# A two-stage encoder block with product-key experts: the first expert table of the last 128 tokens as dot products with fetched rows

## The reference, cut to what matters

```python
def block(tb):                                    # 128 tokens
    qry = (tb @ w_q).reshape(PEER_BLOCK, PEER_HEADS, 2, PEER_HALF)
    s = jnp.einsum('thpd,pkd->thpk', qry, sub_keys)
    sv, si = lax.top_k(s, PEER_TOPK)
    ...
    top, pos = lax.top_k(cand, PEER_TOPK)
    eidx = jnp.take_along_axis(cidx, pos, axis=-1)
    gates = jax.nn.softmax(top.astype(jnp.float32), axis=-1)
    z = jnp.einsum('thed,td->the', expert_u[eidx], tb)
    act = (gates * jax.nn.gelu(z.astype(jnp.float32))).astype(tb.dtype)
    return jnp.einsum('the,thed->td', act, expert_v[eidx])
```

## Time and profile before

| | us |
|---|---|
| runs | 4876.5, 4875.06, 4876.28 (median 4876.28) |
| the profiled execution | 4867.86 |
| its span in the trace | 4866.3 |
| mean granted clock of TensorE | 0.991 of full speed |

### The profile page before, as it was taken

One profiled execution on the slowest core, in us unless ns is written; L12 is line 12 of the kernel. 1 busy time (PEld: TensorE's weight loads), 2 busy tenths in 40 slices (PEclk: granted clock), 3 DMA queues, 4 the chain that ended last, 5 costly groups with the idle time before them and its releaser, 6 DMA issues.

```text
span 4866.3 us, 67163 instructions
## 1 busy us (share of the span) xinstructions
PE 4750.8 (98%) x24576; PEld 4118.7 (85%) x24576; DVE 3004.8 (62%) x4220; ACT 1304.4 (27%) x1287; POOL 698.4 (14%) x741
## 2 busy tenths in 40 slices
PE   8999999999999999999999999999999879999998
PEld 6787888998998888877788888888888879999998
DVE  5555556666665433488788886222224368888886
ACT  4222222212223312212233333222222222223222
POOL 1111110000002001111000000000004732212223
PEclk9999999999999999999999999999999989999999
DMA  4444444555546633322333344333335468888884
GB/s 174 156 162 151 158 156 165 197 196 192 198 144 212 209 135 118 141 78 103 116 142 142 142 177 179 142 118 119 119 119 191 151 236 329 313 326 324 339 305 149
DMA packets 271844, 878.64 MB, mean 181 GB/s; under 512 B 20000, under 2 KB 169920, under 8 KB 197664
## 3 DMA queue, kind: packets, MB, share of 16 engines
q1 hardware_dynamic: 229520, 669.94, 38.3%
q0 software_dynamic: 42256, 207.85, 11.6%
HBM read 802.09 MB, written 209.78 MB: 208 GB/s over the span
## 4 chain that ended last, share of the span: by engine, by line
PE 90%; POOL 3%; DVE 2%; issue 2%; DMA 1%; ACT 0%; DVEq 0%; POOLq 0%; ACTq 0%; SPq 0%
PE bank L632 28%; PE bank L633 28%; PE bank L634 28%; POOL z_pairs L611 3%; DMA w_raw<-v_blocks 1%; PE bank L844 1%; PE bank L732 1%; PE bank L739 1%; DVE w_lo L1252 1%; PE bank L708 1%; PE bank L730 0%; ACT w_hi L905 0%; POOL cand L575 0%; DVE r L1800 0%; PE bank L670 0%
## 5 line engine op out<-in xcount | busy, mean ns | idle before, releaser
L632 PE MATMUL bank<-x_hi,w_hi 128*128 128x512 f32 (+1 forms) x5760 | 2081.1, 361 | 7.1 <-DVE w_lo L1252 7.1
L633 PE MATMUL bank<-x_lo,w_hi 128*128 128x512 f32 (+1 forms) x5760 | 2077.9, 361 | 0.0
L634 PE MATMUL bank<-x_hi,w_lo 128*128 128x512 f32 (+1 forms) x5760 | 2071.7, 360 | 0.0
L905 ACT ACTIVATE w_hi<-w_raw 128x2048 fp32r<-128x2048 f32 x432 | 827.3, 1915 | 2118.4 <-PE bank L634 2066.2
L1252 DVE TENSOR_TENSOR w_lo<-w_raw,w_hi 128x2048 fp32r<-128x2048 f32 x432 | 995.2, 2304 | 542.9 <-ACT w_hi L905 530.8
L632 PEld LDWEIGHTS bank<-x_hi,w_hi 128*128 128x128 f32 x5760 | 1082.9, 188 | 201.5 <-issue 21.3
L633 PEld LDWEIGHTS bank<-x_lo,w_hi 128*128 128x128 f32 x5760 | 1082.4, 188 | 172.1 <-issue 2.6
L634 PEld LDWEIGHTS bank<-x_hi,w_lo 128*128 128x128 f32 x5760 | 1084.0, 188 | 169.6
L632 PE MATMUL bank<-x_hi_o,w_hi 128*128 128x384 f32 x2048 | 687.1, 336 | 63.2 <-DVE w_lo L1252 63.2
L633 PE MATMUL bank<-x_lo_o,w_hi 128*128 128x384 f32 x2048 | 686.1, 335 | 0.3 <-issue 0.3
L634 PE MATMUL bank<-x_hi_o,w_lo 128*128 128x384 f32 x2048 | 686.0, 335 | 0.3 <-issue 0.3
(11 more groups left out here) (263 smaller groups left out, 2665.2 us busy)
## 6 DMA issues: line engine op xcount, KB each, us to landing
v_rows<-v_blocks SPq DMA_DIRECT2D x128, 1024.0 KB, 7.1
w_raw<-u_blocks SPq DMA_DIRECT2D x128, 1024.0 KB
w_raw<-v_blocks SPq DMA_DIRECT2D x128, 1024.0 KB
w_raw<-w_proj SPq DMA_DIRECT2D x112, 1024.0 KB
z_scratch<-z_stage POOLq DMA_DIRECT2D x128, 256.0 KB, 2.3
g_scratch<-g_chunk SPq DMA_DIRECT2D x6, 4096.0 KB, 12.3
z_group<-z_scratch SPq DMA_DIRECT2D x14, 1536.0 KB
g_group<-g_scratch SPq DMA_DIRECT2D x14, 1536.0 KB
```

What stands on the lines that cost most here:

```text
L632: pe.matmul(dst, whi, xhi, start=start, stop=False)
L633: pe.matmul(dst, whi, xlo, start=False, stop=False)
L634: return pe.matmul(dst, wlo, xhi, start=False, stop=stop)
L905: act.activation(WH[s][:, :], RAW[s][:, :], ACT.Copy).then_inc(w_hi, 1)
```

## The change

The last 128 tokens leave the Z stage as they had left the O stage. Their z values become dot products: VectorE multiplies a fetched row of the first table with the token's x row and sums it (`dot`), 128 times. For that:

- The first table is turned to rows in DRAM (`u_rows`), beside the projections: SP loads each of 128 tiles into a free buffer, VectorE transposes it in blocks of 32 x 32 (`u_turn`), SP stores it in four parts (`u_turned`). There is one buffer pair at a time, in four places (a1, a2, b2, c1): 38 tiles in A1, 61 in A2 and the first blocks of B1, 15 in B2 and C1, 14 in C1 and Q1. SP's loops are written out.
- The row copies of the second table are spread anew: one per block of A1, one per two blocks of A2, two per block of B1, one per block of Q1. The sub keys are loaded after A2.
- Z moves 384 columns. x of the last tokens is scaled (ScalarE, Q1), turned by 16 transposes (TensorE, after z block 5) and copied to `x_rows`.
- GpSimd fetches row sets into three buffers, three ahead of the dots. `dots(n)` puts one dot behind each z block 16 to 63 and a second one behind every eighth; after that nine per six blocks, to block 113. The gelu of all pairs is one activation, scaled with a column of 1/rms, before the gelu of z block 120.
- The one-hot products are in fp32, with 128 columns and no low part; the adds from PSUM go; chunks are 32 tokens.
- The 128 pair fetches go. Group 0 is loaded at z block 65, group 1 and the stored h by SP after the last dot. `V_FIRST` is 1. The last tokens' sums, norm and output are separate (`v_sums`, `h_rows`), and the other tokens' final steps have 384 columns.

```diff
-CH = 64
+CH = 32
...
-V_FIRST, V_LAST = 16, 119
+V_FIRST, V_LAST = 1, 119
+QD = P // 32
+U_A1, U_A2, U_B2, U_C1 = 0, 38, 99, 114
+U_A1_X, U_A2_X, U_B2_X, U_C1_X = 6, 52, B2 + 4, C1 + 4
+D_GATE, D_LATE = 9, 9
...
-    z_dram = nc.dram_tensor("z_scratch", (NB_E, P, T), F32, kind="Internal").ap()
+    z_dram = nc.dram_tensor("z_scratch", (NB_E, P, NT), F32, kind="Internal").ap()
...
+    u_rows = nc.dram_tensor("u_rows", (KEYS, QD, 32, QD, KT * 32), F32, kind="Internal").ap()
...
+        def dots(n):
+
+            if n < Z_LOOK + Z_GATE:
+                q, r = divmod(n - Z_LOOK, 8)
+                return [D_GATE * q + r] + ([D_GATE * q + 8] if r == 7 else [])
+            q, r = divmod(n - Z_LOOK - Z_GATE, 6)
+            p0 = D_GATE * Z_GATE // 8 + D_LATE * q
+            return [p for p in range(p0 + 3 * r // 2, p0 + 3 * (r + 1) // 2) if p < P]
...
+            def row_copy(n):
+                jg, d = n // GJ, n % GJ
+                src = v_blocks[n, :, :].rearrange("i (j c) -> i j c", j=GJ)
+                sp.dma_start(v_rows[jg, :, :, d, :], src).then_inc(vr_st, 16)
+
+            def weights(src, n, b0):
+                sp.wait_ge(w_lo, b0 + n + 1)
+                sp.dma_start(RAW[n % 2][:, :], src[n]).then_inc(w_loaded[n % 2], 16)
+
+            def u_load(m, bufs):
+                sp.dma_start(bufs[0][:, :], u_blocks[m]).then_inc(ur_ld, 16)
+
+            def u_turned(m, bufs, more):
+
+                sp.wait_ge(ur_turn, m + 1)
+                for b in range(QD):
+                    sp.dma_start(u_rows[m, b, :, :, :].rearrange("r a n -> a r n"), bufs[1][:, b * D // QD:(b + 1) * D // QD]
+                                 ).then_inc(ur_st[b], 16)
+                if more:
+                    u_load(m + 1, bufs)
+
+            for n in range(2, NB_A1 + NB_A2):
+                weights(w_proj, n, A1)
+                x = n - 2
+                if n < 50:
+                    row_copy(n - 2)
+                elif n % 2 == 0:
+                    row_copy(48 + (n - 50) // 2)
+                if x == U_A1_X - 1:
+                    sp.wait_ge(x_lo, KT)
+                    sp.wait_ge(g_rdy, 1)
+                    u_load(U_A1, u_a1)
+                if U_A1_X <= x < U_A1_X + U_A2 - U_A1:
+                    u_turned(x - U_A1_X + U_A1, u_a1, x - U_A1_X + U_A1 < U_A2 - 1)
+                if x == U_A2_X - 1:
+                    sp.wait_ge(hs_done, 2 * NH)
+                    u_load(U_A2, u_a2)
+                if U_A2_X <= x:
+                    u_turned(x - U_A2_X + U_A2, u_a2, True)
+            sp.wait_ge(hs_done, 2 * NH)
+            sp.dma_start(sk[:], sub_keys).then_inc(sk_ld, 16)
+            row_copy(79)
+            for n in range(NB_16):
+                weights(w_mo, n, B1)
+                for v in range(2):
+                    row_copy(80 + 2 * n + v)
+                x = B1 + n - 2
+                if x < U_A2_X + U_B2 - U_A2:
+                    u_turned(x - U_A2_X + U_A2, u_a2, x - U_A2_X + U_A2 < U_B2 - 1)
...
+            for b0, src in ((B2, w_co), (C1, w_o)):
+                for n in range(NB_16):
+                    weights(src, n, b0)
+                    x = b0 + n - 2
+                    if x == U_B2_X - 1:
+                        sp.wait_ge(x_lo, 48)
+                        u_load(U_B2, u_b2)
+                    if U_B2_X <= x < U_B2_X + U_C1 - U_B2:
+                        u_turned(x - U_B2_X + U_B2, u_b2, x - U_B2_X + U_B2 < U_C1 - 1)
+                    if x == U_C1_X - 1:
+                        sp.wait_ge(x_lo, 64)
+                        u_load(U_C1, u_c1)
+                    if U_C1_X <= x:
+                        u_turned(x - U_C1_X + U_C1, u_c1, True)
...
+            for n in range(NB_16):
+                weights(w_q, n, Q1)
+                x = Q1 + n - 2
+                if x < U_C1_X + KEYS - U_C1:
+                    u_turned(x - U_C1_X + U_C1, u_c1, x - U_C1_X + U_C1 < KEYS - 1)
+                row_copy(112 + n)
...
+            with sp.Fori(0, 26) as i:
+                z_load(Z_LOOK + 4 + Z_GATE + 2 * i)
+
             for s in range(2):
                 sp.wait_ge(g_st[s], 8 * (NT // CH) + 16)
+                sp.wait_ge(z_st[s], 8 * 16)
+            sp.wait_ge(ug_dot, P)
+            group_load(sp, 1, 1, zg_first, gg_first)
             sp.wait_ge(h_st, 16)
             h3 = h_dram.rearrange("p (k t) -> p k t", k=KT)
-            sp.dma_start(R2[:, :, 0:NT], h3[:, :, 0:NT]).then_inc(o_ld, 16)
-            for s in range(2):
-                sp.dma_start(HG[s][:, :, :], h3[:, 8 * s:8 * s + 8, NT:T]).then_inc(hg_ld, 16)
-            with sp.Fori(0, (NB_E - Z_LOOK - 4 - Z_GATE) // 2) as i:
-                z_load(Z_LOOK + 4 + Z_GATE + 2 * i)
+            sp.dma_start(OUT[:, :, :], h3[:, :, 0:NT]).then_inc(o_ld, 16)
+            with sp.Fori(0, 4) as i:
+                z_load(Z_LOOK + 4 + Z_GATE + 52 + 2 * i)
 
...
+            def u_row(p):
+
+                pool.indirect_dma_start(UG[p % VSLOT][:, :], None, u_rows.rearrange("j b r a n -> (j b r) (a n)"),
+                                        bass.IndirectOffsetOnAxis(ap=ZI[:, p:p + 1], axis=0)).then_inc(ug_ld[p % VSLOT], 16)
+
+            def z_stores(n):
+                pool.wait_ge(evac_a, n + 113)
+                pool.dma_start(z_dram[n, :, :], zs[n % 2][:, :]).then_inc(z_st[n % 2], 16)
...
+            pool.wait_ge(ix_rdy, 3)
+            for b in range(QD):
+                pool.wait_ge(ur_st[b], 16 * KEYS)
+            pool.wait_ge(tr_rdy, 3)
+            for p in range(VSLOT):
+                u_row(p)
+            for n in range(Z_LOOK, NB_E):
+                z_stores(n)
+                for p in dots(n):
+                    if p + VSLOT < P:
+                        pool.wait_ge(ug_dot, p + 1)
+                        u_row(p + VSLOT)
+                if n == Z_LOOK + Z_GATE + 1:
+                    for s in range(2):
+                        pool.wait_ge(g_st[s], 8 * (NT // CH) + 16)
+                        pool.wait_ge(z_st[s], 8 * (Z_LOOK + Z_GATE))
+                    group_load(pool, 0, 0, zg_first, gg_first)
...
-            z_flat = z_dram.rearrange("j i t -> (j i t)").unsqueeze(1)
-            for p in range(P):
-                pool.indirect_dma_start(ZP[:, p:p + 1], None, z_flat, bass.IndirectOffsetOnAxis(ap=ZI[:, p:p + 1], axis=0)
-                                        ).then_inc(zp_ld, 16)
...
-                blk(Z1 + n, u, FLAT(bk[u]), [[(z_out, n - 1)]], free=free)
+                blk(Z1 + n, u, [(bk[u], 0, NT)], [[(z_out, n - 1)]], free=free)
...
+            pe.wait_ge(xr_w, KT)
+            for q, bank in enumerate(x_banks):
+                for k in range(4):
+                    m = pe.transpose(bank[:, P * k:P * k + P], r1f[:, (4 * q + k) * T + NT:(4 * q + k) * T + T], ident[:])
+                m.then_inc(xr_rdy, 1)
...
-                        pe.wait_ge(g_add, 8 * i + (4 * u + 2 * g + 2))
+                        pe.wait_ge(g_ev, 4 * i + 2 * u + g + 1)
                         for q in range(4):
-                            m = pe.matmul(A[2 * g + q // 2][:, 2 * P * (q % 2):2 * P * (q % 2) + 2 * P],
-                                          hot_i[g][:, q, :], hot_j[g][:, q, :], start=q % 2 == 0, stop=q % 2 == 1,
-                                          skip_group_check=True)
+                            m = pe.matmul(A[2 * u + g][:, P * q:P * q + P], hot_i[g][:, q, :], hot_j[g][:, q, :],
+                                          start=q == 0, stop=q == 3, skip_group_check=True)
...
+            for k in range(KT):
+                xk = r1f[:, k * T + NT:k * T + T]
+                act.activation(xk, xk, ACT.Identity, scale=col[:, N2W, k:k + 1]).then_inc(xr_w, 1)
...
+            def u_turn(m, bufs):
+
+                dve.wait_ge(ur_ld, 16 * m + 16)
+                if not (isinstance(m, int) and m == 0):
+                    u_stored(m)
+                dve.transpose(bufs[1][:, :].rearrange("p (b k c) -> p b k c", b=QD, c=32),
+                              bufs[0][:, :].rearrange("p (k b c) -> p b k c", b=QD, c=32)).then_inc(ur_turn, 1)
+
+            def u_stored(m):
+                for b in range(QD):
+                    dve.wait_ge(ur_st[b], 16 * m)
...
+                u_turn(6 * h - 4, u_a1)
                 head_norm(h)
-                attention(h)
-                done(NH)
+                u_turn(6 * h - 3, u_a1)
...
+            def dot(p, s, n):
+                dve.wait_ge(ug_ld[s], 16 * n)
+                dve.scalar_tensor_tensor(UG[s][:, :], UG[s][:, :], 1.0, XR[:, :, :, :].rearrange("p a k c -> p (a k c)"),
+                                         ALU.mult, ALU.mult, accum_out=ZP[:, ds(p, 1)]).then_inc(ug_dot, 1)
+
...
+                for b in range(8):
+                    n = 8 * cc + b
+                    for g in range(2):
+                        dve.wait_ge(g_mm, 2 * n + (g + 1))
+                        dve.tensor_tensor(hot_i[g][:, :, :], iota[:, :].unsqueeze(1).to_broadcast((P, 4, P)),
```

(70 more changed lines are left out.)

311 lines of the change are left out of this document (164 added, 147 removed).

## The result

The changed kernel takes 5407.95 us (median of 4 runs, 5404.37 to 5408.92) where the kernel before takes 4875.67 in the same session: 1.109 times as long, 95% interval 1.1071 to 1.111. The forecast was 4531, with 4503 to 4630 as its range and 0.03 for slower. It was wrong by 877 us and in sign.

What follows compares the result with a forecast made beforehand. TensorE, busy 98% of the span, was taken as the bound, so stages cost their matmuls. 172 + 90 + 26 + 68 + 4 - 15 = 345 us off 4876.3 gave 4531, range 4503 to 4630.

Steps and rivals of the forecast that it cites:

- the turning of the table: Beside the projections: 128 loads, VectorE turns of 2.3 us and 512 stores cost 15 us in all.
- The 15 us: Cost of turning the first table beside the projections, 6 of it over fifteen channels; bounds 0 and 100.
- The slower case: Turn at the reciprocal's rate, 13.4 us, holds TensorE in the channel stage and costs 591 us there: 5116 us; 3%.
- price scale: Channel stage: a turn holds TensorE from 3.6 us; loss is fifteen channels x (4 x turn time - 14.2).
- New waits: SP waits for turns, GpSimd for dots; weights behind lose only five transfers' issue time; nothing more while dots keep their blocks.
- Late z blocks: Z stage, 64 blocks moving 384 columns instead of 512, at 8.32 us each: 539 us, gain 172.
- two bursts: Late z: group 0 loaded at block 65, group 1 and sums between weights 119 and 120; 4 and 3 us allowed.
- Gate blocks: Z stage, 48 blocks with eight narrower fp32 one-hot products, 10.16 us each for 12.19: 495 us, gain 90.
- routing: Start of the z stage, VectorE bound first: block 16 starts at 2381 instead of 2407, gain 26, bounds 20 to 30.
- expert stage and end: Expert stage 1070 us for 1138, gain 68 as fetch and gate waits go; final steps with 384 columns gain 4.
- Rival 1: Transfers bind beside the projections: each turn waits about 2.5 us, 78 us lost in channels, some 18 in heads: 4617; 18%.
- The limit of the transfers: Argument against: about 358 GB/s HBM limit per core would make a channel 48 us, the time some 59 more, 4590.

Runs made afterwards that it cites:

- experiment 2: The changed kernel with each turn's four stores cut to 32 partitions and all four column parts (outermost dimension 32), order of issue kept: 4738.4 us.
- experiment 3: The changed kernel with stores of outermost dimension 32 and the next load issued ahead of the stores: 4671.6 us, 0.9592 of the kernel before.
- experiment 5: experiment 3 without the second table's row copies (127 of 128), the last tokens' rows fetched from the table as it lies: 4626.7 us, one run.
- experiment 4: The changed kernel with each store halved, so its outermost dimension is 2 and not 4 (eight stores per turn): 6701.2 us, one run.
- experiment 7: experiment 3 with a second buffer for every second of 40 turns in convolution channels 1 to 10: 4623.7 us, 0.9487 of the kernel before.

## Why the prediction was wrong

**The step that failed** is one clause in the turning of the table: "After a turn, store and next load are 2.1 MB [...] 5.3 to 8.3 us at 398 GB/s plus some 2 of latency". It priced a store by its bytes at the rate of a stretch in which all sixteen engines work. The stores as the change writes them have 4 as their outermost dimension and ran at 90 to 100 GB/s. So the 7 to 10 us became 3.0 of issue and 13.7 until the load was in, against gaps of 8.6 to 10.3, and the loop became 19 us beside blocks of 11.1. The diff showed the shape, `"r a n -> a r n"` with four in front, and the prediction had no row of such a store; 398 GB/s was no bound for it.

With this repaired the step was still too cheap. Experiments 2 and 3, at 4738 and 4672 us, are above the whole range: a loop with spread stores has 2.3 us of issue, which the forecast counted for SyncE alone and not in the loop, and a landing of 6.6 to 10.1 us, as the chains of experiments 3 and 5 have it, before the buffer is free.

The Trainium skill, DMA: Bandwidth & Descriptors, section "Why a DMA increments its semaphore by 16 and not by 1", states the rule that the forecast passed over: a DMA runs on the largest number of engines, up to 16, that divides the slowest dimension of both sides, on this queue the lowest-numbered ones. By it the stores of the change get 4, those of experiment 4 get 2, those of experiment 2 all 16; the shares of 0.26 and 0.13, and 0.86 over 500 us in experiment 2, agree. Which engines they were, no run here shows.

**Bounds and chance.** The 15 us stood between 0 and 100; it was 893. The bounds took in a transfer limit for all traffic together, never one transfer that can't use the engines. The slower case had 3% and a wrong mechanism, the turn as such; the turn took 2.31 us and the dot 2.28, for 2.3 and 2.35 forecast (lines of VectorE, us busy in total, mean ns):

```profile
L1414 DVE STREAM_TRANSPOSE u_turned_a<-u_raw_a 128x2048 f32<-128x2048 f32 x99 | 228.8, 2311 | 879.9 <-DMA u_raw_a<-u_blocks 879.9
...
L1909 DVE SCALAR_TENSOR_TENSOR u_row<-u_row,x_rows 128x2048 f32<-128x2048 f32 x128 | 290.2, 2284 | 0.0
```

Its price scale was usable all the same. A turn that waits holds VectorE's queue as a long turn would: in the 60 blocks of the convolution it waited 569.7 us, 9.5 a turn, and with its own 2.3 that is 11.8. By the forecast's formula that is 15 x (4 x 11.8 - 14.2) = 495 us, an estimate; the convolution took 477 more.

**New waits.** That the weights "lose only the issue time of five transfers" held for SyncE with spread stores and not as written: the weights w_proj land in 10.6 us (median) in the kernel after, in 6.3 with spread stores and the copies moved, and in 5.1 with spread stores and no copies. TensorE's 513 us of waits for splits can be of both kinds, turns that hold VectorE and weights that come late. In the convolution they are 362.5 us, and there ScalarE, which takes the weights first, waited only 56.7 us for `w_proj`; so most of it seems to be the turns, though no run parts the two.

**What held.** Late z blocks: 172 forecast, 169 measured. The period is 8.45 and not 8.32, which is 8 us over 64 blocks and stands in the place of the 7 allowed for two bursts. TensorE is busy 541.7 of 543 us there, so it is not a wait; why these products take longer than those of the expert stage is open. Two ends of such blocks on VectorE:

```profile
4268.12 0.56 DVE L1825 TENSOR_TENSOR z_stage<-bank,rstd_b 128x384 f32<-128x384 f32 x1 [4.21 <-PE bank L743]
...
4276.57 0.56 DVE L1825 TENSOR_TENSOR z_stage<-bank,rstd_b 128x384 f32<-128x384 f32 x1 [4.21 <-PE bank L743]
```

Gate blocks 90 and 85; routing 26 and 23; expert stage and end 72 and 74; TensorE waits 0.5 us for splits in the expert stage. Together 360 and 352. Turns, loads and their effect on TensorE: 15 and 9. The forecast's 4523 for a profiled execution is 4524.6 in the run without stores; part of that is luck, as errors of 8 and 6 us cancel.

**Rival 1**, transfers that bind beside the projections (4617, each turn waiting 2.5 us), describes the repaired kernel: experiment 3 has 13.2 us a convolution block (789.7 / 60) where it had 49.6 / 4 = 12.4. But traffic is only a part of its cause: 45 us go with the copies, and 48 with a second buffer at the same traffic. Whether the two gains add was not tried.

**The limit of the transfers.** The prediction had weighed the 358 GB/s that the Trainium skill, DMA: Bandwidth & Descriptors, section "Where 436 GB/s comes from", gives as a core's limit with HBM. In the stretch of experiment 7 the core moved 327 GB/s. The trace counts a copy once: over the whole run the profile has 1273 MB moved, but 1070 read from HBM and 336 written to it, and the difference of 133 MB is the 128 copies. 21 row copies begin in the stretch, 1.05 MB each in 500 us, another 44 GB/s. By this estimate 371 GB/s went to and from HBM with TensorE busy 98.5%, so that limit did not bind here either.

## What to carry to other kernels

Before a transfer is priced by its bytes, look at the outermost dimension of both its sides: here 4 meant the work of four engines, and the load issued behind took 13.7 us to land. Cut such a transfer the other way; the same bytes, pieces and addresses in stores of 32 partitions were worth 670 us here. Then follow a single buffer once around (turn, issues, landing, release): if that loop is longer than the block beside it, a free engine does not help. Leaving the row copies out gave 45 us here, and a second buffer for 40 of the turns 48.

## What was not expected of the hardware

A DMA with 4 or 2 as its outermost dimension ran at a DMA share of 0.26 or 0.13 and at 90 to 100 or 51 GB/s, and with several of them issued it went no higher. Their issue grows as well: in experiment 4 the eight stores of one turn took SyncE 0.49, 0.48, 0.66, 0.67, 2.42, 1.16, 4.34 and 2.48 us, against 0.43 to 0.92 for the spread ones in the chains of experiments 3 and 5. The medians of all are 0.99 and 0.44 us. What holds SyncE there, no row shows. And an idle TensorE costs twice: in the 1173 us of the convolution it was busy 780 us for products that took 696 before, at a mean granted clock of 0.83 and not 1.00:

```profile
997.00:2170.00 1173.00, 780.39 (x4237) 693.41 (x4238) 602.76 (x648) 152.75 (x134) 63.67 (x48) 0.83 0.57 202
```

What is still open: the 99 us (4623.7 less 4524.6) between the second-buffer version and the run without stores. In the profiled executions 26 us lie ahead of the first convolution sum, 43 in the convolution and 28 from there to the z stage. The turns still wait 277 us for the stores of the turn before (192.4, 36.6 and 48.0 by buffer). That a second buffer there would recover the 99 us was not tried.
